# Placing the rows and the shared expert: two blocks made one, with the block words computed among the tiles

## The chip, the cores and the metric

The kernel runs on one core of one Trainium2 chip. The metric is the time of one execution on the device in microseconds (us). Five engines matter, and each works through its own queue in order: TensorE (PE, with PEld for its weight loads), VectorE (DVE), ScalarE (ACT), GpSimd (POOL) and SyncE (SP), which here only issues DMAs. They wait for each other on semaphores. A DMA issued by SP or ACT is cut into packets and spread over 16 DMA engines.

## What is computed

One decoder layer over 2048 tokens of width 1024: a mixer (sliding-window attention beside a gated recurrence), LayerNorm, then a mixture of experts with a shared expert, LayerNorm again. The change lies in the mixture, between the routing and the routed experts:

```python
    counts = jnp.bincount(flat_e, length=N_EXPERTS)
    padded = (counts + MOE_BLOCK - 1) // MOE_BLOCK * MOE_BLOCK
    pad_end = jnp.cumsum(padded)
    pad_start = pad_end - padded
    ...
    dest = pad_start[sorted_e] + (jnp.arange(n_pairs, dtype=jnp.int32) - sort_start[sorted_e])
    row_token = jnp.full((n_rows,), n_tok, jnp.int32).at[dest].set(flat_tok[order])
    block_expert = jnp.minimum(
        jnp.searchsorted(pad_end, jnp.arange(n_blocks) * MOE_BLOCK, side='right'), N_EXPERTS - 1)
    ...
    shared = (jax.nn.silu(hf @ ws_gate) * (hf @ ws_up)) @ ws_down
    return (acc[:n_tok] + shared.astype(f32)).astype(h.dtype).reshape(bsz, seq, dm)
```

Each token goes to 8 of 64 experts. The (token, expert) pairs are sorted by expert into blocks of 128 rows, each expert padded to whole blocks, at most 192 blocks.

## The kernel before

The program is a row of blocks; at the end of one all engines meet before the next begins. `mixer` takes the first 638 us, `output_and_route` the next 283 us. It leaves, per token, `mask` (the experts chosen) and `cum` (running counts), and writes the normalised rows to HBM twice: `htab` by rows (with the routing weights) and `hT_d` transposed. Behind the change stand `experts` (the routed experts, 164 blocks here) and `final_norm`.

Between them stand the two blocks that the change touches.

`place_rows` (L1202) computes positions. DVE casts `mask` and the triangle `tri` to bf16 (L1302, L1304), PE multiplies them into counts (`psCnt`) and ranks (`psRank`, L1276 to L1281), and DVE then goes through one chain of small linked operations, each waiting for the one before: block counts and ends per expert (L1308 to L1315), the block words, that is which expert each of the 192 blocks belongs to (L1317 to L1342), the position of each pair (`dm`, `d8`, `dpf`, `dbf`, `tv`, L1348 to L1359) and the table (L1365 on). Meanwhile ACT copies the shared expert's weights to rounded values `s_gu` and `s_d` in six pieces (L1291), and POOL subtracts to get the low parts, one operation for each piece (L1257). SP loads the first routed expert's weights (`prefetch_first`, 3 MB).

`shared_and_dispatch` (L1372) goes over the 16 tiles of 128 tokens with a two-deep loop (`two_deep`, L804): in the turn of tile n the engines do the head of tile n+1 and the tail of tile n. On PE a tile is 24 gate/up matmuls (L1556, high by high, high by low, low by high), the transposes of H (L1570), eight dispatch matmuls that add the token numbers into `psD` by one-hot matrices (L1574), and 12 down matmuls (L1584). On ACT: `hT_hi` (L1481), `sg` (L1491), `HT_hi` (L1496). On DVE: `hT_lo` (L1504), H (L1517), `HT_lo` (L1521), 16 one-hot operations (L1528, L1529), `out` (L1537). SP issues, in this order, the loads of `hT` for tiles 0 and 1, of `h`, the zeroing of the pad rows of `htab` and `acc` (L1442, L1443), the second routed expert's weights (`prefetch_second`, 3 MB, L1595), and only then the load of `hT` for tile 2. When the last dispatch is in, DVE writes `idx` (L1544), on which the routed experts' gathers wait.

## Time and profile before

| | |
|---|---|
| median of 3 runs | 2778.65 us (2766.59 to 2778.68) |
| profiled execution | 2779.59 us, its span 2777.4 us |
| `place_rows` in it | 921.4 to 953.3 us of the span |
| `shared_and_dispatch`, to `idx` | 953.3 to 1123.6 us |
| first matmul of the routed experts | 1132.6 us |
| TensorE busy | 2573.1 us (93%) |

Times in rows are microseconds from the start of the span unless marked ns. In a timeline row the first number is the start, the second how long the (merged) group took, then engine, line, operation, out<-in, how many, and in brackets how long the engine had been idle and who ended that. `SPq` rows are issues of DMAs. The granted clock of TensorE stands in the windows view as a share of full speed: 0.50 is 1.2 GHz, 1.00 is 2.4 GHz.

### The profile page before, as it was taken

To read this page: it belongs to the slowest core of one execution; us is meant where nothing else is said; L and a number is where in the kernel's file an instruction comes from. 1 tells how busy PE (TensorE), PEld (TensorE's weight loads), DVE (VectorE), ACT (ScalarE), POOL (GpSimd) and SP (SyncE) were. 2 spreads that over 40 slices of the span, in tenths; PEclk is the share of its full clock that TensorE was granted. 3 is DMA by queue.
4 is the path that set the end of the run, shared out by engine and by line. 5 is a ranking of instruction groups with operands and counts; after the bars stand their busy time and mean duration, and the time that the engine had idled before them with its cause. 6 is when DMAs were issued, how large, how long until landed. Compare 5 with 4: busy or idle time off the path is not lost. (4 is left out here: it accounts for less than half of the span.)

```text
span 2777.4 us, 50926 instructions
## 1 busy us (share of the span) xinstructions
PE 2573.1 (93%) x11862; PEld 1981.7 (71%) x11863; DVE 1547.3 (56%) x2691; ACT 1184.0 (43%) x1791; POOL 737.6 (27%) x825
## 2 busy tenths in 40 slices
PE   8999999997988399799999999999999999999990
PEld 4555656465777278688888888888888888888880
DVE  2544434354888667565556555565566555655535
ACT  2424343343343111454455544455555444554425
POOL 0000000001121200234344433344334333543335
PEclk9999998998999599999999999999999999999995
DMA  5010101005333444687888888789888877988656
GB/s 182 4 57 0 60 0 56 4 11 206 146 131 124 167 157 153 201 263 231 240 230 273 260 240 230 224 266 276 245 253 253 239 221 220 280 255 240 162 117 265
DMA packets 253806, 495.95 MB, mean 179 GB/s; under 512 B 24272, under 2 KB 166736, under 8 KB 253776
## 3 DMA queue, kind: packets, MB, share of 16 engines
q1 hardware_dynamic: 202816, 313.29, 32.8%
q0 software_dynamic: 47808, 179.59, 25.7%
q10 hardware_dynamic: 3152, 2.72, 0.3%
q8 instruction: 12, 0.20, 0.0%
q14 instruction: 18, 0.15, 0.0%
HBM read 366.02 MB, written 129.53 MB: 178 GB/s over the span
## 5 line engine op out<-in xcount | busy, mean ns | idle before, releaser
L1784 POOL DMA_INDIRECT acc<-y,si x164 | 293.2, 1788 | 759.5 <-DMA acc<-y,si 333.0
L1873 DVE TENSOR_TENSOR gu_lo<-raw_gu,gu_hi (+1 forms) x128 | 292.9, 2289 | 175.3 <-ACT gu_hi L1804 156.1
L1981 PE MATMUL psG<-gu_hi,xT_lo 128*128 x1320 | 348.5, 406 | 0.4 <-issue 0.3
L1970 PE MATMUL psG<-gu_hi,xT_hi 128*128 x1328 | 338.6, 397 | 3.1 <-ACT xT_hi L1800 3.1
L1970 PE MATMUL psG<-gu_lo,xT_hi 128*128 x1328 | 336.1, 395 | 0.0
L1970 PEld LDWEIGHTS psG<-gu_hi,xT_hi 128*128 128x128 f32 x1328 | 250.6, 189 | 64.1 <-issue 3.8
L1970 PEld LDWEIGHTS psG<-gu_lo,xT_hi 128*128 128x128 f32 x1328 | 250.0, 188 | 60.4
L1981 PEld LDWEIGHTS psG<-gu_hi,xT_lo 128*128 128x128 f32 x1320 | 236.7, 189 | 45.4 <-issue 1.4
L1804 ACT ACTIVATE gu_hi<-raw_gu (+1 forms) x128 | 238.3, 1910 | 45.6 <-issue 45.6
L623 PE MATMUL psP<-xT,win 128*128 128x512 f32 x512 | 236.0, 618 | 3.2 <-DMA win<-in_w_in_dram 3.2
L1760 POOL DMA_INDIRECT xg<-htab,gi x168 | 200.7, 1195 | 140.9 <-POOL gi L1757 125.8
L1873 DVE TENSOR_TENSOR d_lo<-raw_d,d_hi (+1 forms) x64 | 146.7, 2293 | 152.1 <-ACT d_hi L1804 149.4
L1853 ACT ACTIVATE HT_hi<-psH 128x256 fp32r<-128x256 f32 x164 | 63.1, 385 | 382.0 <-PE psH L1988 382.0
L1870 DVE TENSOR_TENSOR xT_lo<-psX,xT_hi 128x512 fp32r<-128x512 f32 x332 | 212.8, 683 | 8.8 <-ACT xT_hi L1800 8.7
L1942 DVE COPY y<-psY 128x512 f32<-128x512 f32 x164 | 112.9, 689 | 179.5 <-PE psY L2026 166.1
L2026 PE MATMUL psY<-d_hi,HT_hi 128*128 x656 | 207.0, 397 | 0.0
L2026 PE MATMUL psY<-d_lo,HT_hi 128*128 x656 | 206.3, 396 | 0.0
L2026 PE MATMUL psY<-d_hi,HT_lo 128*128 x656 | 206.3, 395 | 0.0
L623 PEld LDWEIGHTS psP<-xT,win 128*128 128x128 f32 x512 | 99.7, 199 | 122.9 <-issue 122.6
L1800 ACT ACTIVATE xT_hi<-psX 128x512 fp32r<-128x512 f32 x332 | 180.8, 597 | 10.4 <-PE psX L1954 1.9
L1954 PE MATMUL psX<-ident,xg 128*128 128x128 f32 x1336 | 174.1, 273 | 10.1 <-DMA xg<-htab,gi 10.1
L634 PE MATMUL psP<-win,xT 128*128 128x256 f32 (+1 forms) x512 | 171.2, 489 | 0.0
(291 smaller groups left out, 3903.4 us busy)
## 6 DMA issues: line engine op xcount, KB each, us to landing
raw_gu<-in_w_gate_dram SPq DMA_DIRECT2D x64, 1024.0 KB, 6.0
raw_gu<-in_w_up_dram SPq DMA_DIRECT2D x64, 1024.0 KB
raw_d<-in_w_down_dram SPq DMA_DIRECT2D x64, 1024.0 KB
xs<-in_x_dram SPq DMA_DIRECT2D x20, 512.0 KB, 4.2
htab<-row SPq DMA_DIRECT2D x16, 544.0 KB, 2.7
mT<-mixed SPq DMA_DIRECT2D x16, 512.0 KB, 5.4
xt<-in_x_dram SPq DMA_DIRECT2D x16, 512.0 KB, 5.8
hT_d<-hT SPq DMA_DIRECT2D x16, 512.0 KB, 3.9
```

The lines of the kernel that those rows point to most:

```text
L623: m = nc.tensor.matmul(b.tile[:], win[:, k, col:col + P], xT[:, k, :], start=(k == 0), stop=(k == KC - 1))
L634: m = nc.tensor.matmul(b.tile[:, 0:n], xT[:, k, t * P:(t + 1) * P], win[:, k, col:col + n], start=(k == 0), stop=(k == KC - 1))
L1760: nc.gpsimd.indirect_dma_start(out=xg[slot][:], out_offset=None, in_=htab, in_offset=bass.IndirectOffsetOnAxis(ap=gi[slot][:, 0:1], axis=0 ...
L1784: nc.gpsimd.indirect_dma_start(out=acc, out_offset=bass.IndirectOffsetOnAxis(ap=si[k][:, 0:1], axis=0), in_=y[k][:], in_offset=None, compu ...
L1800: nc.scalar.activation(xT_hi[slot][:, h * HALF:(h + 1) * HALF, :], psX[h][:], ACT.Copy).then_inc(xhi_s[h], 1)
L1804: nc.scalar.activation(dst, src, ACT.Copy).then_inc(done, 1)
L1870: nc.vector.tensor_tensor(xT_lo[slot][:, at, :], psX[h][:], xT_hi[slot][:, at, :], ALU.subtract).then_inc(xlo_s[h], 1)
L1873: nc.vector.tensor_tensor(dst, src, hi, ALU.subtract).then_inc(dlo_s if n == 2 else gulo_s, 1)
L1954: m = nc.tensor.transpose(psX[half][:, c, :], xg[slot][:, (half * HALF + c) * P:(half * HALF + c + 1) * P], ident[:])
L1970: nc.tensor.matmul(psG[slot][:], xT_hi[slot][:, c, :], right[:, bass.ds(w, 1), c, :].rearrange("p a n -> p (a n)"), start=(n == 0 and c == ...
L1981: m = nc.tensor.matmul(psG[slot][:], xT_lo[slot][:, c, :], gu_hi[:, bass.ds(w, 1), c, :].rearrange("p a n -> p (a n)"), start=False, stop= ...
L2026: m = nc.tensor.matmul(psY[:, h, :], left[:, c, :], right[:, bass.ds(w, 1), c, h * 512:(h + 1) * 512].rearrange("p a n -> p (a n)"), start ...
```

## The change

Both functions become one, `place_and_share`, with one block and no meeting of the engines between. The loops over the 16 tiles are written out in Python, so that the program holds all 16 tiles one after the other. The same arithmetic is done; what differs is order and place:

- DVE: `hT_lo` of tile 0 comes ahead of the expert starts, then `tri` (half as wide: the constant ones are now set on chip), then `hT_lo` of tile 1 and the positions. The block words stand behind the tiles 4 to 7, the table behind tile 9. `dm` uses the buffer of `out[1]`.
- PE: the count and rank matmuls stand ahead of the tiles; the rank matmuls wait for `tri` (`tri_s`). The dispatch of tile n-1 stands where that of tile n stood. Gate/up takes its parts as high by high, low by high, high by low, and in tile 0 waits piece by piece for the weights.
- ACT: `hT_hi` of tile 0, then the four gate/up pieces, `hT_hi` of tile 1, the two down pieces.
- SP: `hT` of tile 0 first; the pad rows are zeroed from a 64-wide column of zeros read again and again; `hT` of tiles 2 and 3 is issued ahead of `prefetch_second`; in the loop `hT` is loaded four tiles ahead.

```diff
+            load_hT(0)
+            sp.dma_start(trif[:], tri_h[:, 0, :]).then_inc(consts_in, 16)
...
+            load_hT(1)
+            load_h(0)
+            load_h(1)
+            sp.dma_start(htab[SEQ:ROWS, :].rearrange("p (a b) -> p a b", b=EXPERTS),
+                         bcast(zeros, 1, ROW_W // EXPERTS)).then_inc(pads_out, 16)
...
+            prefetch_first(sp)
+            load_hT(2)
+            load_hT(3)
+            sp.wait_ge(shared_hi_s, PIECES)
+            sp.wait_ge(shared_lo_s, PIECES)
+            prefetch_second(sp)
...
+            low(0)
+            expert_starts()
+            dve.wait_ge(consts_in, 48)
+            nc.vector.tensor_copy(tri[:], trif[:]).then_inc(tri_s, 1)
...
+            low(1)
+            positions()
+            dve.wait_ge(late_in, 48)
+            product(0)
+            for n in range(TILES):
+                if n + 2 < TILES:
+                    low(n + 2)
+                if n + 1 < TILES:
+                    product(n + 1)
+                low_HT(n)
+                one_hot(n)
+                finish(n)
+                if n == 4:
+                    ranks_of_used()
+                elif n in (5, 6):
+                    block_words(n - 5)
+                elif n == 7:
+                    codes()
+                elif n == 9:
+                    write_table()
...
+            pe.wait_ge(tri_s, 1)
...
+            gate_up(0)
+            for n in range(TILES):
+                if n + 1 < TILES:
+                    gate_up(n + 1)
+                turn_H(n)
+                if n:
+                    dispatch(n - 1)
+                if n == 9:
+                    pe.wait_ge(be_s, 1)
...
+                down(n)
+            dispatch(TILES - 1)
```

`low`, `product`, `low_HT`, `one_hot` and `finish` are the DVE steps L1504, L1517, L1521, L1528/1529 and L1537 of before.

The order on DVE where the placing begins, before (the casts, then straight into the chain; `bend` are the block ends):

```order
L1302 CAST maskb<-mask 128x1024
L1304 CAST tri<-trif 128x256
L1305 MEMSET one 128x64
L1308 TENSOR_SCALAR nbi<-psCnt 128x64
L1309 TENSOR_SCALAR nbj<-nbi 128x64
L1310 CAST nb<-nbj 128x64
L1311 SCALAR_TENSOR_TENSOR bend<-one,nb 128x64
L1313 TENSOR_SCALAR used<-nb 128x64
```

The same place on DVE after:

```order
L1506 CAST maskb<-mask 128x1024
L1507 MEMSET ones 128x128
L1508 MEMSET one 128x64
L1405 TENSOR_TENSOR hT_lo<-hT_0,hT_hi 128x1024
L1439 TENSOR_SCALAR nbi<-psC 128x64
L1440 TENSOR_SCALAR nbj<-nbi 128x64
L1441 CAST nb<-nbj 128x64
L1442 SCALAR_TENSOR_TENSOR bend<-one,nb 128x64
L1443 TENSOR_TENSOR bs<-bend,nb 128x64
L1444 TENSOR_SCALAR bst<-bs 128x64
L1512 CAST tri<-trif 128x128
L1513 CAST zr<-cum 128x192
```

The cast of `tri` has moved from the second place to the place behind six operations of the chain and the low part of tile 0.

The order on PE from the counts to the first down matmuls, before:

```order
L1276 MATMUL psCnt<-cumb,tri 128x64
L1280 MATMUL psRank<-maskb,tri 128x512
L1281 MATMUL psRank<-cumb,tri 128x512
L1280 MATMUL psRank<-maskb,tri 128x512
L1281 MATMUL psRank<-cumb,tri 128x512
L1284 MATMUL psRow<-ident,code 1x128 x2
L1207 UNCONDITIONAL_BRANCH
L1547 UNCONDITIONAL_BRANCH
L1556 MATMUL psG<-s_gu,hT_hi 128x512 x16
L1556 MATMUL psG<-s_gu,hT_lo 128x512 x8
```

And after:

```order
L1542 MATMUL psC<-cumb,ones 128x64
L1547 MATMUL psRank<-maskb,tri 128x512
L1548 MATMUL psRank<-cumb,ones 128x512
L1547 MATMUL psRank<-maskb,tri 128x512
L1548 MATMUL psRank<-cumb,ones 128x512
L1560 MATMUL psG<-s_gu,hT_hi 128x512 x8
L1560 MATMUL psG<-s_gu,hT_lo 128x512 x8
L1560 MATMUL psG<-s_gu,hT_hi 128x512 x16
L1560 MATMUL psG<-s_gu,hT_lo 128x512 x8
L1560 MATMUL psG<-s_gu,hT_hi 128x512 x8
L1570 MATMUL psH<-ident,H_0 128x128 x2
L1596 MATMUL psY<-s_d,HT_hi 128x512 x4
```

The code matmuls (`psRow`) and the meeting of the engines between ranks and gate/up are gone; the first gate/up matmul stands right behind the four rank matmuls, which read `tri`.

The order on SP around the weights of the second expert, before:

```order
L1431 DMA hT_0<-hT_d 128x1024
L1431 DMA hT_1<-hT_d 128x1024
L1434 DMA h_0<-htab 128x1024
L1434 DMA h_1<-htab 128x1024
L1442 DMA htab<-zero 128x1088
L1443 DMA acc<-zero 128x1024
L1595 DMA raw_gu<-in_w_gate_dram 128x8x256
L1595 DMA raw_gu<-in_w_up_dram 128x8x256
L1595 DMA raw_d<-in_w_down_dram 128x2x1024
L1431 DMA hT_0<-hT_d 128x1024
```

And after (the first group of three is the first expert, the second the second):

```order
L1314 DMA h_1<-htab 128x1024
L1327 DMA htab<-cum 2176x1x64
L1329 DMA acc<-cum 2048x1x64
L1619 DMA raw_gu<-in_w_gate_dram 128x8x256
L1619 DMA raw_gu<-in_w_up_dram 128x8x256
L1619 DMA raw_d<-in_w_down_dram 128x2x1024
L1308 DMA hT_0<-hT_d 128x1024
L1308 DMA hT_1<-hT_d 128x1024
L1619 DMA raw_gu<-in_w_gate_dram 128x8x256
L1619 DMA raw_gu<-in_w_up_dram 128x8x256
L1619 DMA raw_d<-in_w_down_dram 128x2x1024
L1318 DMA acc<-out_0 128x1024
```

The loads of `hT` for tiles 2 and 3 now stand ahead of the second expert's weights, but behind the first expert's and behind two zeroing transfers of 2176 and 2048 runs of 64 elements.

## Rows read from the trace of the kernel before

**Rows 1.** The page's first section: busy time of each engine.
```profile
PE 2573.1 (93%) x11862; PEld 1981.7 (71%) x11863; DVE 1547.3 (56%) x2691; ACT 1184.0 (43%) x1791; POOL 737.6 (27%) x825
```

**Rows 2.** Windows: busy time (instructions) by engine, granted clock, DMA share, GB/s.
```profile
921.40:953.30 31.90, 2.95 (x9) 0.82 (x9) 25.37 (x69) 6.80 (x7) 13.90 (x6) 0.50 0.40 134
953.30:972.90 19.60, 14.73 (x59) 11.85 (x59) 6.94 (x20) 3.79 (x4) 1.00 (x1) 0.76 0.93 328
972.90:983.50 10.60, 4.69 (x12) 3.71 (x13) 5.35 (x18) 2.55 (x4) 0.00 (x0) 0.68 0.27 107
983.50:1113.10 129.60, 129.60 (x627) 106.60 (x625) 91.47 (x263) 21.32 (x38) 0.00 (x0) 1.00 0.47 159
```

**Rows 3.** Timeline of the placing: DVE's chain beside POOL's low parts.
```profile
923.59 9.31 POOL L1257 TENSOR_TENSOR s_gu<-raw_gu,s_gu 128x1024 fp32r<-128x1024 f32 x4 [20.35 <-ACT s_gu L1291]
...
928.81 0.23 DVE L1308 TENSOR_SCALAR nbi<-psCnt 128x64 int32<-128x64 f32 x1 [0.33 <-PE psCnt L1276]
...
929.07 1.58 DVE L1309 TENSOR_SCALAR nbj<-nbi 128x64 int32<-128x64 int32 x1
...
935.38 2.17 DVE L1313 TENSOR_SCALAR used<-nb 128x64 f32<-128x64 f32 x1
...
937.91 0.22 DVE L1315 TENSOR_TENSOR bs<-bend,nb 128x64 f32<-128x64 f32 x1
```

**Rows 4.** Timeline in the routing: a DVE operation with two SBUF inputs beside POOL.
```profile
845.26 2.54 POOL L990 TENSOR_TENSOR mT_lo<-mT,mT_hi 128x1024 fp32r<-128x1024 f32 x1 [2.78 <-ACT mT_hi L1013]
...
845.59 3.29 DVE L1089 TENSOR_TENSOR row<-row,bias 128x1024 f32<-128x1024 f32 x1
```

**Rows 5.** Windows: the rank matmuls, the block words, the positions.
```profile
928.40:930.40 2.00, 1.94 (x5) 0.49 (x5) 1.63 (x4) 0.00 (x0) 2.00 (x1) 0.50 1.07 373
938.60:944.00 5.40, 0.00 (x0) 0.00 (x0) 4.70 (x20) 0.00 (x0) 0.00 (x0) 0.50 0.00 0
945.50:951.90 6.40, 0.74 (x4) 0.15 (x2) 6.06 (x26) 0.00 (x0) 0.00 (x0) 0.50 0.00 0
```

**Rows 6.** Timeline where the shared expert begins.
```profile
953.30 0.82 SPq L1431 DMA_DIRECT2D hT<-hT_d  x2
...
957.04 1.06 ACT L1481 ACTIVATE hT_hi<-hT 128x1024 fp32r<-128x1024 f32 x1 [28.79 <-DMA hT<-hT_d]
...
958.15 6.08 PE L1556 MATMUL psG<-s_gu,hT_hi 128*128 128x512 f32 x16 [11.92 <-ACT hT_hi L1481]
```

**Rows 7.** Timeline around the stall of tile 0.
```profile
965.87 2.34 SPq L1431 DMA_DIRECT2D hT<-hT_d  x2
...
977.06 1.06 ACT L1481 ACTIVATE hT_hi<-hT 128x1024 fp32r<-128x1024 f32 x1 [10.53 <-DMA hT<-hT_d]
...
978.81 2.04 PE L1584 MATMUL psY<-s_d,HT_hi 128*128 128x512 f32 x4 [5.92 <-ACT HT_hi L1496]
```

**Rows 8.** Timeline of PE in the steady loop: one tile.
```profile
1002.72 3.90 PE L1556 MATMUL psG<-s_gu,hT_hi 128*128 128x512 f32 x16
...
1009.41 1.11 PE L1584 MATMUL psY<-s_d,HT_hi 128*128 128x512 f32 x4
...
1012.22 3.90 PE L1556 MATMUL psG<-s_gu,hT_hi 128*128 128x512 f32 x16
```

**Rows 9.** Timeline of the end: last gate/up, output of tile 14, the index.
```profile
1111.06 2.03 PE L1556 MATMUL psG<-s_gu,hT_lo 128*128 128x512 f32 x8
...
1118.08 1.23 DVE L1537 SCALAR_TENSOR_TENSOR out<-h,psY 128x1024 f32<-128x1024 f32 x1
...
1123.60 0.41 DVE L1544 TENSOR_SCALAR idx<-psD,pad 128x192 int32<-128x192 f32 x1
```

**Rows 10.** DMA queues (packets, MB, share of 16 engines): 639 to 651, then 921 to 936.
```profile
q10 hardware_dynamic: 1165, 0.32, 11.8%
...
q1 hardware_dynamic: 3216, 4.43, 88.2%
```

More of the change, by code:

```diff
@@ L1475, in _ @@
-            act.dma_start(pad[:], pad_h).then_inc(consts_in, 16)
-            def high(s):
-                s.wait_slot(act, hT_in, per=16)
-                s.wait_two_behind(act, gu_s)
-                nc.scalar.activation(hT_hi[s.slot][:], hT[s.slot][:], ACT.Copy).then_inc(hThi_s, 1)
-            high(Step(0, 0))
-            def head(s):
-                if not (isinstance(s.n, int) and s.n == TILES - 1):
-                    high(s.next())
-                s.wait(act, gu_s)
-                s.wait(act, H_s, behind=1)
-                nc.scalar.activation(sg[:], psG[s.slot][:, 0:FE], ACT.Silu).then_inc(silu_s, 1)
@@ L1519, in low_HT, with link, low, product @@
-            def low_HT(s):
-                s.wait(dve, HThi_s)
+            done = [0]
+            def link(ins):
+                done[0] += 1
+                ins.then_inc(seq, 1)
+                dve.wait_ge(seq, done[0])
+            def low(n):
+                dve.wait_ge(hThi_s, n + 1)
+                nc.vector.tensor_tensor(hT_lo[n % 2][:], hT[n % 2][:], hT_hi[n % 2][:], ALU.subtract).then_inc(hTlo_s, 1)
+            def product(n):
+                dve.wait_ge(silu_s, n + 1)
+                if n >= 2:
+                    dve.wait_ge(HTps_s, n - 1)
+                nc.vector.tensor_tensor(H[n % 2][:], sg[:], psG[n % 2][:, FE:2 * FE], ALU.mult).then_inc(H_s, 1)
@@ new lines, in ranks_of_used @@
+            def ranks_of_used():
+                link(nc.vector.tensor_scalar(used[:], nb[:], 0.0, None, ALU.is_gt))
+                link(nc.vector.tensor_tensor_scan(out=rank[:], data0=one[:], data1=used[:], initial=0.0, op0=ALU.mult, op1=ALU.add))
+                link(nc.vector.tensor_scalar(last_block[:, 0:1], bend[:, EXPERTS - 1:EXPERTS], -1.0, None, ALU.add))
+                dve.wait_ge(late_in, 48)
+                link(nc.vector.tensor_scalar(bclamp[:], blockno[:], last_block[:, 0:1], None, ALU.min))
@@ new lines, in _ @@
+            nc.tensor.matmul(psC[:, 0:EXPERTS], ones[:], cumb[:, TILES, :], start=True, stop=True).then_inc(count_s, 1)
+            pe.wait_ge(tri_s, 1)
+            for hf in range(2):
+                t8 = slice(hf * 8, hf * 8 + 8)
+                o = psRank[:, t8, :].rearrange("p t e -> p (t e)")
+                nc.tensor.matmul(o, tri[:], maskb[:, t8, :].rearrange("p t e -> p (t e)"), start=True, stop=False)
+                nc.tensor.matmul(o, ones[:], cumb[:, t8, :].rearrange("p t e -> p (t e)"), start=False, stop=True).then_inc(count_s, 1)
@@ L1575, in tail, with down @@
                                          skip_group_check=True)
                 m.then_inc(disp_s, 1)
-                s.wait(pe, out_s, behind=1)
-                s.wait(pe, HThi_s)
+            def down(n):
+                if n:
+                    pe.wait_ge(out_s, n)
+                else:
+                    pe.wait_ge(shared_hi_s, PIECES)
+                    pe.wait_ge(shared_lo_s, PIECES)
+                pe.wait_ge(HThi_s, n + 1)
                 for hf in range(2):
-                    for n, (left, part) in enumerate(((HT_hi, 0), (HT_hi, 1), (HT_lo, 0))):
-                        if n == 2 and hf == 0:
-                            s.wait(pe, HTlo_s)
+                    for part, (left, right) in enumerate(((HT_hi, 0), (HT_hi, 1), (HT_lo, 0))):
+                        if part == 2 and hf == 0:
+                            pe.wait_ge(HTlo_s, n + 1)
@@ L1583, in tail @@
                         for c in range(2):
-                            m = nc.tensor.matmul(psY[:, hf, :], left[:, c, :], s_d[:, part, c, hf * 512:(hf + 1) * 512],
-                                                 start=(n == 0 and c == 0), stop=(n == 2 and c == 1))
+                            m = nc.tensor.matmul(psY[:, hf, :], left[:, c, :], s_d[:, right, c, hf * 512:(hf + 1) * 512],
+                                                 start=(part == 0 and c == 0), stop=(part == 2 and c == 1))
```

406 lines of the change are left out of this document (195 added, 211 removed).

## The prediction, made before the changed kernel was run

> **What bounds the kernel now.** The page's busy times come first: TensorE is busy for 93% of the span [rows 1], so whatever does not keep it from working is worth nothing. The windows by stage show where it is kept from working [rows 2]. In the steady loop of the shared expert, 983.5 to 1113.1, it is busy for all of 129.60 us at the full clock (1.00, 2.4 GHz): a tile costs 9.50 us, from one gate/up start to the next [rows 8], and nothing that DVE or ACT saves there can show. In the 31.9 us of the placing it works 2.95 us [rows 2]; between 972.9 and 983.5 it does 12 matmuls in 10.6 us. So there are two holes: the placing, in which everyone waits for a chain on DVE, and a stall at tile 0. The question is how early TensorE can begin the gate/up matmuls (I call that time S; it is 958.15 before [rows 6]) and how much of the road from S to the index at 1123.60 [rows 9] is kept. The index starts the routed experts, which are bound by TensorE and unchanged, so what is won there is kept to the end.
>
> **When TensorE starts now.** The first gate/up matmul stands behind the four rank matmuls, and these wait for the cast of `tri`, which DVE does behind the low part of tile 0 and six operations of the chain. So S is DVE's time for these, plus the rank matmuls. What does DVE meet there [rows 3]? While POOL makes the low parts (four pieces in 9.31 us, 2.33 us each; six pieces busy 13.90 us [rows 2]), DVE's `nbj` takes 1.58 us and ends at 930.65, `used` takes 2.17 us and ends at 937.55, where POOL has just ended its last piece; between them stand two more of the same kind. An operation that reads PSUM (`nbi`, 0.23 us at 928.81) isn't held, and once POOL is done a 128x64 operation takes 0.22 us. So beside POOL each such operation on DVE ends with POOL's present piece: one per piece. That one with two SBUF inputs is held as well is seen in the routing [rows 4]: `row<-row,bias` takes 3.29 us beside a piece of POOL that began just ahead of it. In the new order nbj, nb, bend, bs, bst and tri are six operations of these kinds, and POOL has six pieces. I take it that `tri` ends with POOL's last piece.
>
> Step by step: the load of `hT` for tile 0 is the first issue at 921.4, and `hT_hi` followed such an issue by 3.74 us [rows 6]; the stores of the routing are still under way, so 4.1: 925.5. ACT takes 1.06 for `hT_hi`, then about 1.0 for the first weight piece (six pieces are most of its 6.80 us [rows 2]): POOL starts at 927.6. Six pieces, 13.9 us: 941.5. The cast ends some 0.2 later, 941.7. The rank matmuls take 2.0 us [rows 5]: **S = 943.8**, 14.35 us earlier than before. Bounds: with the small `bs` and `bst` not held, one or two pieces less, 941.5 at the earliest of this kind; with `hT` landing 2 us later, 945.8. The middle is taken since both kinds are seen held [rows 3, 4].
>
> The positions (6.06 us of DVE work [rows 5]) follow the rank matmuls, behind the low part of tile 1, and block H of tile 0, for which TensorE asks only after the gate/up of tiles 0 and 1. Before, 59 matmuls from 958.15 ended at 972.9, of which the last ten are dispatch and turning, 1.3 us: two gate/ups at the start took 13.4 us, slow clock of the beginning included [rows 2, 6]. 6.4 us lie within that 13.4. Cost 0; without that cover it would be 6.4.
>
> **From S to the index.** Before it is 1123.60 - 958.15 = 165.45 us [rows 6, 9]. The same TensorE work is done, so I change only what differs.
>
> Stall, -7.8. ACT waits 10.53 us for the `hT` of tile 2, which landed 11 us after its issue at 965.87, behind the second expert's 3 MB, and `HT_hi` of tile 0 stands behind it on ACT; the down matmuls start at 978.81 [rows 7]. They take 2.8 us in the steady loop (1009.41 to 1012.22 [rows 8]) and here the stretch is 10.6 us [rows 2], at clock 0.68, since TensorE fell to 1.2 GHz in the wait. 10.6 - 2.8 = 7.8.
>
> Does the new order keep `hT` of tile 2 early? It must be in ACT before the gate/up of tile 1 ends, S + 13.4 - 1.06 = 956.1. From 921 on SP's queue moved 4.43 MB in 15 us, 295 GB/s [rows 10]. Now four loads of 0.52 MB stand in it as well: 6.5 MB, 22 us, 943.1; its own 0.5 MB 1.8 us: 944.9, plus P, the price of zeroing the pads in 2176 + 2048 pieces of 256 bytes, 264 for each of 16 DMA engines. No row shows writes of that size. Nearest is the queue with the router weights, 1165 packets of 275 bytes in the mean, 11.8% of 16 engines for 12 us [rows 10]: 19 ns a packet, P = 5.1. The upper end is the mean packet of the second row there (1378 bytes): 88.2% of 240 us by 3216, 66 ns, P = 17.4. I take 5.1, since the size is the same: landing at 950.0, 6.1 us early. The spare time is used up at 42 ns a packet.
>
> The Trainium skill ("DMA: Bandwidth & Descriptors", Specifications) states that below 512 bytes a DMA engine does a read-modify-write. These zeroing writes are 256 bytes, so the rule speaks against this edit; the row of small packets is a load and can't tell. If that doubled the 19 ns, P would be 10.2 and still inside the spare time; a rival below carries the case where it isn't.
>
> New gap at tile 0, +0.6: no dispatch stands between its turning and its down matmuls, and ACT's `sg` and `HT_hi` lie bare there. In all later tiles the dispatch of the tile before fills it. Code matmuls in tile 9, +0.5: in the placing they fell in a wait, now they stand in TensorE's queue; beside the positions they show as 0.74 us at clock 0.50 [rows 5], with weight loads about 1.0, halved at the full clock.
>
> Block words on DVE: 20 operations, 4.70 us [rows 5], with ranks, codes and table about 7.6 us over tiles 4 to 9. DVE is busy 91.47 of 129.60 us in the steady loop [rows 2], free 2.8 us in 9.5, some 17 us over six tiles. Behind the two heaviest tiles (2.4 us each) it is at most level. What queues behind them is the low part of a tile two ahead and H of the next, neither of which TensorE wants at once. Cost 0, bound 1; wholly bare it would be 7.6.
>
> End, +1.4. The last gate/up ended at 1113.09 and the index came 10.5 us later [rows 9]. Now DVE has the output of tile 14 (ends 1119.3, +6.2) ahead of the whole one-hot of tile 15 (about 3.9 us with `HT_lo` 4.3), and then dispatch and closing matmul (1.3): 6.2 + 4.3 + 1.3 = 11.8 to 11.9.
>
> SP's waits: the second expert's load waits for both the first expert's landing and POOL, and the store of tile 0 and the load of tile 4 queue behind it; that store is first ready near 963, the first expert landed near 950. Cost 0. Writing the loops out: no row shows a loss at the loop's edges (129.60 of 129.60), so no gain either.
>
> **Sum.** 943.8 + 165.45 - 7.8 + 0.6 + 0.5 + 1.4 = 1103.95, against 1123.60: 19.65 us less. 2779.59 - 19.65 = 2759.9 for the profiled execution. It lies 0.9 above the median of its runs, so 2759 stands for a median. A measurement of this kernel tells some 0.5% (14 us) from no change.
>
> **Rivals.**
> 1. *DVE isn't held.* The six operations take 0.3 each, `tri` is ready near 930, S = 932.0, 11.8 earlier. Then the gate/up of tile 1 ends at 945.4 and `hT` of tile 2 (950.0, due by 944.3) is late by 5.7: 11.8 - 5.7 = 6.1 more gain, 2753. Against it: four of four were held [rows 3]. For it: POOL may start later than I think.
> 2. *Small packets at 66 ns.* P = 17.4, `hT` of tile 2 lands 6.2 late, a part of the old stall returns: 2765.
> 3. *The block words are bare.* DVE's extra 7.6 us pushes TensorE: 2766.6. Against it is the free 2.8 us a tile.
> 4. *Slower: the zeroing writes cost like full packets.* 4096 bytes at 295 GB/s over 16 engines is 222 ns; 264 of them are 58.6 us, `hT` of tile 2 lands 47 us late, with ACT, H and TensorE behind it: 2759 + 47 = 2806. It is slower than before from P = 11.2 + 19.65 = 31 us on, 117 ns a packet, six times the nearest row.
>
> **How the numbers follow.** Forecast 0.78, rival 1 0.08, rival 2 0.06, rival 3 0.05, rival 4 0.03. Of the forecast's 0.78 I give 0.04 to gains below 14 us, since S may be 2 us late and the three runs of before lie 12 us apart. Faster 0.74 + 0.08 = 0.82, same 0.04 + 0.06 + 0.05 = 0.15, slower 0.03. The range takes in rivals 1 to 3 and the terms' bounds with some scatter of runs: 2746 to 2769.
>
> **What would show it.** The first gate/up matmul at about 944, right behind the rank matmuls, with PE waiting for `tri` until 941.7; DVE's six operations of about 2.3 us each beside POOL; no wait of ACT for `hT` of tile 2; tiles of 9.50 us at clock 1.00; the index near 1104. Wrong would be a first gate/up near 932, an `hT` of tile 2 landing after 956, or tiles 5 to 7 longer than 9.5.

## The result, and the profile after

The changed kernel takes **2761.58 us** in the median of 15 runs (2753.14 to 2764.11), the kernel before 2778.36 in 15 runs on the same chip: a ratio of 0.9937, 95% interval 0.9924 to 0.9951. That is some 17 us less (14 to 21 by the interval), where the prediction said 19.65. Both profiled executions say where: the span went from 2777.4 to 2758.8 us, 18.6 less, and the index from 1123.60 [rows 9] to 1104.58, 19.0 less. What follows the index takes 1654.2 us, before 1653.8, so nothing was won or lost there.

The first section of the changed kernel's page, its busy times, for [rows 1]:

```profile
PE 2568.1 (93%) x11861; PEld 1979.8 (72%) x11863; DVE 1548.6 (56%) x2691; ACT 1181.7 (43%) x1791; POOL 725.6 (26%) x824
```

TensorE's work is the same within 5 us; the span is shorter by idle time alone. The windows by stage, for [rows 2] (span and length; busy time and instructions of PE, PEld, DVE, ACT, POOL; granted clock; DMA share; GB/s):

```profile
921.60:946.20 24.60, 1.13 (x4) 0.57 (x6) 17.08 (x13) 10.07 (x10) 14.03 (x6) 0.50 1.02 312
946.20:958.90 12.70, 12.70 (x50) 10.13 (x49) 7.68 (x27) 1.33 (x2) 0.00 (x0) 0.88 0.91 314
958.90:968.40 9.50, 8.88 (x40) 6.99 (x39) 6.90 (x20) 1.60 (x3) 0.00 (x0) 1.00 0.24 78
968.40:1092.00 123.60, 123.60 (x602) 101.91 (x601) 95.59 (x294) 21.31 (x38) 0.00 (x0) 1.00 0.48 161
```

The two holes of before (31.9 and 10.6 us) have become one of 24.6 us at the start; from 946.20 on TensorE has work. The timeline of that hole, for [rows 3] and [rows 6] (start, duration, engine, line, operation, and in brackets the idle time before it with what ended it):

```profile
921.59 0.52 SPq L1308 DMA_DIRECT2D hT<-hT_d  x1
...
928.65 1.06 ACT L1365 ACTIVATE hT_hi<-hT 128x1024 fp32r<-128x1024 f32 x1 [3.60 <-DMA hT<-hT_d]
...
930.73 9.43 POOL L1351 TENSOR_TENSOR s_gu<-raw_gu,s_gu 128x1024 fp32r<-128x1024 f32 x4 [27.31 <-ACT s_gu L1382]
...
930.96 0.22 DVE L1439 TENSOR_SCALAR nbi<-psC 128x64 int32<-128x64 f32 x1
931.21 2.09 DVE L1440 TENSOR_SCALAR nbj<-nbi 128x64 int32<-128x64 int32 x1
933.34 2.28 DVE L1441 CAST nb<-nbj 128x64 f32<-128x64 int32 x1
...
942.55 2.29 DVE L1512 CAST tri<-trif 128x128 bf16<-128x128 f32 x1
...
946.23 3.54 PE L1560 MATMUL psG<-s_gu,hT_hi 128*128 128x512 f32 x8
```

`hT` of tile 0 is there 7.0 us after its issue. POOL starts a piece later, and then six operations of DVE last 2.1 to 2.4 us each where `nbi`, which reads PSUM, takes 0.22; `tri` ends with POOL's last piece. The first gate/up follows the rank matmuls at 946.23.

Tile 0, for [rows 7], and the end, for [rows 9]:

```profile
953.81 1.05 ACT L1365 ACTIVATE hT_hi<-hT 128x1024 fp32r<-128x1024 f32 x1
...
958.90 0.38 PE L1570 MATMUL psH<-ident,H 128*128 128x128 f32 x2
...
959.90 1.16 PE L1596 MATMUL psY<-s_d,HT_hi 128*128 128x512 f32 x4 [0.62 <-ACT HT_hi L1377]
...
1090.77 2.03 PE L1560 MATMUL psG<-s_gu,hT_hi 128*128 128x512 f32 x8
...
1097.81 1.21 DVE L1432 SCALAR_TENSOR_TENSOR out<-h,psY 128x1024 f32<-128x1024 f32 x1
...
1104.58 0.42 DVE L1536 TENSOR_SCALAR idx<-psRank,pad 128x192 int32<-128x192 f32 x1 [0.22 <-PE psRank L1613]
```

ACT takes `hT` of tile 2 without a wait (no bracket on its row); the down matmuls start 0.62 us after the turning; 123.60 of 123.60 us are busy at clock 1.00; and the index comes 11.8 us behind the last gate/up.

### The profile page after: what moved, and what is told of

It reads as the page before. It is cut to its first block and busy times, and to the rows that moved or that the text cites. A ratio compares the mean times of both kernels' runs of the same rounds, so it can differ in the third digit from the quotient of the medians.

```text
span 2758.8 us, 50465 instructions
## 1 busy us (share of the span) xinstructions
PE 2568.1 (93%) x11861; PEld 1979.8 (72%) x11863; DVE 1548.6 (56%) x2691; ACT 1181.7 (43%) x1791; POOL 725.6 (26%) x824
## 5 line engine op out<-in xcount | busy, mean ns | idle before, releaser
L1897 DVE TENSOR_TENSOR gu_lo<-raw_gu,gu_hi (+1 forms) x128 | 292.7, 2287 | 175.0 <-ACT gu_hi L1828 158.4
L1784 POOL DMA_INDIRECT xg<-htab,gi x168 | 190.1, 1132 | 138.8 <-POOL gi L1781 131.4
L1978 PE MATMUL psX<-ident,xg 128*128 128x128 f32 x1336 | 174.1, 274 | 8.8 <-DMA xg<-htab,gi 8.8
```

Source lines behind the costliest of these rows:

```text
L1784: nc.gpsimd.indirect_dma_start(out=xg[slot][:], out_offset=None, in_=htab, in_offset=bass.IndirectOffsetOnAxis(ap=gi[slot][:, 0:1], axis=0 ...
L1897: nc.vector.tensor_tensor(dst, src, hi, ALU.subtract).then_inc(dlo_s if n == 2 else gulo_s, 1)
L1978: m = nc.tensor.transpose(psX[half][:, c, :], xg[slot][:, (half * HALF + c) * P:(half * HALF + c + 1) * P], ident[:])
```

## The experiments

Stages ahead of this one take a few microseconds more or less from one profiled execution to the next: the first load of the stage is issued between 916.1 and 925.1 in kernels that are alike up to there. So stretches are compared. This table has them for the changed kernel and all that are built on it, in us: from that issue (`hT` of tile 0) to the first gate/up (S), from S to the index, and both together; then the ratio of the timed runs to those of before.

| kernel | issue at | to S | S to index | sum | ratio (95%) |
|---|---|---|---|---|---|
| changed kernel | 921.59 | 24.6 | 158.4 | 183.0 | 0.9937 (0.9924, 0.9951) |
| changed kernel again | 919.13 | 24.1 | 159.0 | 183.1 | 0.9928 (0.9902, 0.9954) |
| tri first | 923.96 | 9.8 | 167.3 | 177.1 | 0.9915 (0.9884, 0.9947) |
| no low parts | 922.19 | 12.1 | 164.7 | 176.8 | 0.9915 (0.9887, 0.9942) |
| words ahead | 919.74 | 24.2 | 161.9 | 186.2 | 0.9953 (0.9929, 0.9978) |
| wide zeros | 924.25 | 24.3 | 157.9 | 182.2 | 0.9944 (0.9925, 0.9962) |
| narrow zeros | 922.51 | 24.3 | 157.9 | 182.2 | 0.9916 (0.9884, 0.9948) |
| late constants | 925.07 | 18.5 | 158.4 | 176.9 | 0.9907 (0.9875, 0.9938) |
| own tile | 923.03 | 24.2 | 157.2 | 181.4 | 0.9924 (0.9899, 0.9949) |
| parts on VectorE | 916.14 | 7.3 | 166.8 | 174.1 | 0.9895 (0.9859, 0.9930) |
| the same, own tile | 916.87 | 7.1 | 166.6 | 173.7 | 0.9915 (0.9886, 0.9943) |
| the same, late second weights | 924.73 | 7.5 | 158.3 | 165.8 | 0.9849 (0.9823, 0.9874) |

Two runs of the changed kernel agree within 0.1 us in the sum and 0.6 us in its parts: from S to the first turning it takes 12.7 us in one and 13.5 in the other, for TensorE stays at half its clock for longer in the second (0.50 over the first 4.0 us, against 0.58 over the first 3.5). Differences below 1 us in one part are therefore not told from none. Moreover, the two runs with other zeros, whose sums are equal, have medians 6.7 us apart (2762.19 and 2755.50). Verdicts of a few microseconds therefore rest on the stretches, each read from one profiled execution.

**1. Is DVE held by POOL? `tri` cast first.**

```diff
-            low(0)
-            expert_starts()
             dve.wait_ge(consts_in, 48)
             nc.vector.tensor_copy(tri[:], trif[:]).then_inc(tri_s, 1)
             nc.vector.tensor_copy(zr[:]...).then_inc(zr_s, 1)
+            low(0)
+            expert_starts()
```

> The changed kernel with one move: the casts of tri and zr stand ahead of the low part of tile 0 and of the expert starts on DVE. Theory (the start of the gate/up matmuls is set by tri, which stands behind six DVE operations that POOL holds back): the rank matmuls are done by about 931.5 instead of 946.2; the gate/up of tile 0 then runs at the pace of POOL's low parts and ends near 942 instead of 953; the low part of tile 1 and the positions now end last on DVE, H of tile 0 comes at about 953.8, five us before the 958.9 of the changed kernel; index at about 1099.5 instead of 1104.6, time about 2757 (5 less than the changed kernel). Rival (something else than tri holds TensorE, the weights' low parts): tri is early, but the gate/up of tile 0 still ends near 953 and the time stays 2761.

The timeline of this run, DVE, POOL and PE at the start of the stage:

```profile
932.17 0.23 DVE L1510 CAST tri<-trif 128x128 bf16<-128x128 f32 x1 [7.25 <-DMA ident<-in_ident_h_dram]
933.05 10.00 POOL L1351 TENSOR_TENSOR s_gu<-raw_gu,s_gu 128x1024 fp32r<-128x1024 f32 x4 [27.26 <-ACT s_gu L1382]
933.78 3.97 PE L1560 MATMUL psG<-s_gu,hT_hi 128*128 128x512 f32 x8
...
943.10 2.59 PE L1560 MATMUL psG<-s_gu,hT_hi 128*128 128x512 f32 x10 [1.58 <-POOL s_gu L1351]
...
945.48 3.29 DVE L1405 TENSOR_TENSOR hT_lo<-hT,hT_hi 128x1024 fp32r<-128x1024 f32 x1
948.82 3.52 PE L1560 MATMUL psG<-s_gu,hT_lo 128*128 128x512 f32 x8 [3.13 <-DVE hT_lo L1405]
```

Ahead of POOL's first piece the same cast takes 0.23 us in place of 2.29. TensorE's first gate/up starts 14.8 us sooner, but doesn't keep that: it waits for POOL's low pieces (1.58 us) and then for the low part of tile 1 (3.13 us), which DVE, held in the chain, made late. The index is 5.9 us earlier. TensorE waits once more at the turning of tile 0, 1.34 us for H. So the held operations are real and are what bounds S; behind them POOL's 14 us of low parts is the next bound.

**2. The same from the other side: no low parts.** POOL fills the tiles with zeros instead; the low parts of the shared weights are left out of the result.

```diff
-                pool.wait_ge(shared_hi_s, n + 1)
-                nc.gpsimd.tensor_tensor(lo, raw, hi, ALU.subtract)...
+                nc.gpsimd.memset(lo.bitcast(F), 0.0)...
```

> The changed kernel, with POOL's six low parts of the shared weights replaced by six memsets to zero that wait for nothing: the low parts of the shared expert's weights are left out of the computation. Theory (POOL's two-input operations hold DVE): DVE's nbj, nb, bend, bs, bst and tri take 0.2 to 0.4 us each instead of 2.1 to 2.4, tri is ready near 933, the first gate/up matmul starts at about 934.7 instead of 946.2; then hT of tile 2 (landed at 947.9 in the changed kernel) is the next thing to be late, down matmuls of tile 0 near 950 instead of 959.9, index near 1095, time about 2752. Rival (these operations are slow by themselves or for the DMA traffic): they stay above 2 us each and the first gate/up matmul stays at 946.

The timeline of this run, two of DVE's operations, then ACT and PE at tile 0:

```profile
931.36 0.19 DVE L1439 TENSOR_SCALAR nbj<-nbi 128x64 int32<-128x64 int32 x1
...
932.63 0.23 DVE L1511 CAST tri<-trif 128x128 bf16<-128x128 f32 x1
...
949.94 1.06 ACT L1364 ACTIVATE hT_hi<-hT 128x1024 fp32r<-128x1024 f32 x1 [7.94 <-DMA hT<-hT_d]
...
951.68 2.04 PE L1595 MATMUL psY<-s_d,HT_hi 128*128 128x512 f32 x4 [4.31 <-ACT HT_hi L1376]
```

With POOL idle `nbj` takes 0.19 us and `tri` 0.23, and S comes 12.6 us earlier. This is rival 1 of the prediction, made to happen: `hT` of tile 2 is now late (ACT waits 7.94 us), and TensorE waits 4.31 us for `HT_hi` behind it. 6.4 us of the gain go back (the sum is 6.2 us shorter; this kernel's index, expected near 1095, comes at 1099.0). That is near that rival's 5.7, but made up otherwise: the wait is only 3.7 us longer than the 0.62 of the changed kernel, and the other 2.7 us are TensorE at half its clock behind it (0.50 from 951.7 to 957.0; the first four down matmuls take 2.04 us in place of 1.16), which the rival's working left out.

**3. What was the stall of tile 0 worth? The kernel before, with `hT` of tile 2 issued ahead of the second expert's weights.**

```diff
+            load(Step(0, 0))
             prefetch(sp)
-            loads_ahead(sp, TILES, load, store_and_load, store)
+            loads_ahead(sp, TILES, load, store_and_load, store, True)
```

> The kernel before with one move: the load of hT for tile 2 is issued ahead of the second expert's weights. Theory (the stall of tile 0 is the queueing of that load behind 3 MB): the wait of ACT for it, 10.5 us, is gone, the down matmuls of tile 0 start at about 973.5 instead of 978.8 and at the full clock, the index comes 7.8 us earlier (near 1116), time 7.8 below the kernel before, ratio 0.997. Rival (the stall only moves to the next load, hT of tile 3, still behind the weights): index within 2 us of 1123.6.

The timeline of this run, ACT and PE at tile 0:

```profile
973.80 1.06 ACT L1482 ACTIVATE hT_hi<-hT 128x1024 fp32r<-128x1024 f32 x1 [2.27 <-DMA hT<-hT_d]
...
977.74 1.11 PE L1585 MATMUL psY<-s_d,HT_hi 128*128 128x512 f32 x4
```

The down matmuls follow the dispatch without a gap, where they waited 5.92 us before [rows 7]. From S to the index it is 156.9 us in place of 165.45: the stall was worth 8.5 us by that stretch, and 8.2 between the turnings of tiles 0 and 1 alone (9.52 us in place of 17.67); the forecast's term was 7.8. The rival is out: the next tile takes 9.50 us, so the stall has not moved on. Of the 19 us that the change won, this one edit of a load's place would have won 8.5; the timed runs show it weakly (0.9979, 0.9957 to 1.0001).

**4. Are the block words covered? All of them ahead of the loop.**

```diff
             positions()
             dve.wait_ge(late_in, 48)
+            ranks_of_used()
+            block_words(0)
+            block_words(1)
+            codes()
             product(0)
```

> The changed kernel with the ranks, block words and codes put back ahead of the tiles, behind the positions. Theory (among the tiles they lie in DVE's free time; ahead of them only part of their 7 us finds cover under the gate/up of tiles 0 and 1): H of tile 0 at about 960.6, TensorE 1.7 to 2.2 us late at its turning, the tiles after it as before, index about 1106.6 and time about 2763.6, 2 more than the changed kernel. Rival (moving the words was the larger part of the gain): the full 7 us come back, index near 1111.5.

The timeline of this run on PE, at the turning and the down matmuls of tile 0:

```profile
958.92 0.41 PE L1568 MATMUL psH<-ident,H 128*128 128x128 f32 x2 [2.49 <-DVE H L1411]
...
959.89 2.04 PE L1594 MATMUL psY<-s_d,HT_hi 128*128 128x512 f32 x4 [0.57 <-ACT HT_hi L1377]
```

Its window (length, PE busy with instructions, granted clock, DMA share, GB/s) over those down matmuls:

```profile
959.90:962.60 2.70, 2.70 (x7) 0.50 0.00 0
```

Ahead of `product(0)` the words are bare: TensorE waits 2.49 us for H, and the down matmuls then run at clock 0.50. S to index is 3.6 us longer, 1.6 more than expected: 2.3 us lie ahead of the turning, as expected, and 1.4 between it and the next (10.84 us in place of 9.48), where the clock is low. Among the tiles they cost nothing: with them tiles 5 and 6 of the changed kernel take 9.48 and 9.49 us, the same as those without.

**5 and 6. What does a small packet cost? The pads zeroed from a tile as wide as a row, and in pieces of 64 bytes.**

```diff
-  sp.dma_start(htab[SEQ:ROWS, :]... b=EXPERTS), bcast(zeros, 1, ...))
+  sp.dma_start(htab[SEQ:ROWS, :], zero[:])                     # wide
+  sp.dma_start(htab[SEQ:ROWS, :]... b=16), bcast(zeros[:, 0:16], 1, ...))  # narrow
```

> The pads of htab and acc are written from a zero tile that is as wide as a row, so that 64 or so elements are no longer one packet of 256 bytes: 4,224 small packets become a few hundred large ones. The tile is zeroed on POOL at the start of the stage, before its low parts. Main theory (a small packet costs about 19 ns, together some 5 us of all 16 queues' time): hT of tile 2 lands 2 to 5 us earlier than the 947.85 of the changed kernel, still ahead of its use at 958, so that the time stays at 2761.6 (within 3 us); a POOL memset ahead of the low parts may cost up to 1 us at the first gate/up. Rival (a small packet costs 66 ns or more): hT of tile 2 lands over 10 us earlier. Rival (the pads cost nothing beside the loads): it lands where it did.

> The pads of htab and acc are written in pieces of 64 bytes: 16,896 packets in place of 4,224, the bytes the same. Main theory (a packet's price hardly depends on its size when it is small, about 19 ns): four times the packets are 20 us of all 16 queues' time in place of 5, so hT of tile 2 lands some 11 to 16 us later than 947.85, near or past the 958 at which it is needed, and the time is 0 to 6 us above the changed kernel (2761.6 to 2768). Rival (zeroing writes cost like full packets, 222 ns): over 200 us of the queues' time, tens of microseconds later. Rival (the price goes by bytes): nothing changes.

Packets of all queues from 915 to 975, with wide zeros:

```profile
DMA packets 7669, 14.26 MB, mean 238 GB/s; under 512 B 816, under 2 KB 5296, under 8 KB 7666
```

The same with narrow zeros; the changed kernel has 5,008 packets under 512 bytes:

```profile
DMA packets 24126, 13.56 MB, mean 226 GB/s; under 512 B 17696, under 2 KB 22176, under 8 KB 24123
```

Its timeline on ACT, the high part of tile 2:

```profile
957.92 1.06 ACT L1365 ACTIVATE hT_hi<-hT 128x1024 fp32r<-128x1024 f32 x1 [3.81 <-DMA hT<-hT_d]
```

Measured from the first issue, `hT` of tile 2 lands at 26.3 us in the changed kernel, at 24.9 with wide zeros (1.4 us sooner, where 2 to 5 was expected) and at 35.4 with narrow ones. 12,672 more packets, 792 for each of 16 DMA engines, cost 9.1 us: **11.5 ns each** at equal bytes. 4,192 packets under 512 bytes fewer save 1.4 us, 5.3 ns each, when the bytes stay. These are prices of cutting the same bytes smaller; the 19 ns of the forecast was the whole time of a packet of 256 bytes, bytes included. That is read where hardly anything else is under way. The changed kernel from 933 to 936:

```profile
DMA packets 2713, 0.69 MB, mean 231 GB/s; under 512 B 2712, under 2 KB 2712, under 8 KB 2713
```

And the narrow zeros from 937 to 943:

```profile
DMA packets 7933, 0.51 MB, mean 84 GB/s; under 512 B 7933, under 2 KB 7933, under 8 KB 7933
```

2,713 packets in 3 us on 16 engines are 17.7 ns for each of 256 bytes, and 7,933 in 6 us 12.1 ns for each of 64. So the 19 ns, read from loads of 275 bytes, held nearly for these writes, while rival 2 (66 ns) and rival 4 (222 ns) were far off. The expectation for the narrow zeros (11 to 16 us later) was too high because it kept 19 ns for a packet a fourth as long. Neither run moves the time, since even the narrow one lands just as TensorE comes to need it: S to index is 157.9 us in both. The timed ratios, 0.9944 and 0.9916, differ by less than their intervals. On the read-modify-write below 512 bytes of the Trainium skill ("DMA: Bandwidth & Descriptors", Specifications) these runs say only that such zeroing writes stay cheap here; whether one took place they can't show.

**7. Why did `hT` of tile 0 take 7.0 us? ACT's three constants issued behind the high part of tile 0.**

```diff
-            act.dma_start(iota[:], bcast(iota_h, 0, P))...
-            act.dma_start(blockno[:], blockno_h)...
-            act.dma_start(pad[:], pad_h)...
             nc.scalar.activation(cumb[:], cum[:], ACT.Copy)...
             high(0)
+            (the same three issues)
```

> ACT issues iota, blockno and pad behind the high part of tile 0 instead of ahead of it, while SP issues its own transfers; nothing else moves. It tests why hT of tile 0 took 7.0 us from issue to landing in the changed kernel, where 4.1 had been forecast. Theory (it shares queues and issue time with the constants around it): hT of tile 0 lands 1 to 3 us sooner after its issue, and the first gate/up starts 1 to 3 us sooner; time 2759 to 2761. Rival (the landing goes by the row copies and big loads that are under way anyway): the landing stays at 7 us and the time at 2761.6.

The timeline of this run, ACT, DVE and POOL at the start:

```profile
929.99 1.06 ACT L1362 ACTIVATE hT_hi<-hT 128x1024 fp32r<-128x1024 f32 x1 [3.78 <-DMA hT<-hT_d]
...
932.54 0.19 DVE L1440 TENSOR_SCALAR nbj<-nbi 128x64 int32<-128x64 int32 x1
932.82 9.28 POOL L1351 TENSOR_TENSOR s_gu<-raw_gu,s_gu 128x1024 fp32r<-128x1024 f32 x4 [25.92 <-ACT s_gu L1382]
933.00 2.34 DVE L1442 TENSOR_TENSOR_SCAN bend<-one,nb 128x64 f32<-128x64 f32 x1
...
939.89 2.29 DVE L1512 CAST tri<-trif 128x128 bf16<-128x128 f32 x1
```

The load now lands 4.9 us after its issue, 2.1 sooner. That three issues of ACT stand beside it can't be the whole cause, for in the kernel before they stood there too, and `hT` landed after 3.74 us [rows 6]. The timeline of before, ACT's issues:

```profile
953.31 0.36 ACTq L1473 DMA_DIRECT2D ident<-in_ident_h_dram  x1
953.70 0.46 ACTq L1474 DMA_DIRECT2D iota<-in_iota_h_dram  x1
```

A third, `pad`, follows at 954.18. What differs is that there the stores of the routing had long landed, and here they are under way (403 GB/s from 921.6 to 923.0, against 77 from 953.3 to 955.0). So with the stores the load takes some 1.2 us longer (4.9 against 3.74), and with stores and constants 3.3. Why the two together cost so much isn't shown.

S gains 6.1 us, three times as much, which neither theory had said. The rows show why. ACT's three issues now stand between `hT_hi` and its first weight piece, so POOL begins 2.83 us after `hT_hi` began, in the changed kernel 2.08. DVE's `nbj` begins 2.55 us after `hT_hi` in both. So here it is ahead of POOL's first piece and takes 0.19 us, `nb` too (0.20); only four operations are held, not six, and `tri` ends with POOL's fourth piece. A shift of 0.75 us between POOL's start and DVE's chain was worth two pieces of POOL. This wasn't tried by itself; the reading rests on these rows and on runs 1 and 2.

**8. Dispatch in its own tile again.**

```diff
+            one_hot(0)
             product(0)
...
                 low_HT(n)
-                one_hot(n)
+                if n + 1 < TILES:
+                    one_hot(n + 1)
...
-                if n:
-                    dispatch(n - 1)
+                dispatch(n)
```

> The dispatch of a tile stands in its own tile again, between hidden and the turn of H, with one_hot made a tile ahead; all else of the changed kernel stays. Theory (the gap of 0.6 us between the end of turn_H(0) and down(0) is there since dispatch(0) no longer fills it, and the last dispatch hangs behind the last tile): no gap at tile 0, and from the end of the last gate/up to idx 10.4 us in place of 11.8; together 2 us less, about 2759.6. Rival (a dispatch between hidden and the turn of H waits for one_hot or for the code): tiles get longer than 9.49 us, by 0.1 us each already 1.6 us in all, which eats it: 2761.6 or more.

The timeline of this run on PE, dispatch and down matmuls of tile 0:

```profile
960.41 1.05 PE L1582 MATMUL psRank<-OB,OP 128*128 128x192 f32 x8
961.30 1.11 PE L1598 MATMUL psY<-s_d,HT_hi 128*128 128x512 f32 x4
```

No gap at tile 0, tiles of 9.48 us, and the last turning is followed by the index after 6.8 us in place of 8.0. From the first turning to the index it is 144.3 us in place of 145.7 and 145.5 in the two runs of the changed kernel: 1.2 to 1.4 us gained, not 2. From the first turning to the last nothing is: 137.5 us, and 137.6 in the changed kernel. The gap that is filled takes in the work of one more dispatch within the tiles, and only the tail is won. The expectation counted both.

**9 to 11. Put together.** The first eight runs say that S is bounded by `hT` of tile 0, then by POOL; so POOL gets no work and VectorE makes the low parts, ACT the high parts ahead of `hT`.

```
 ACT  cumb, then the four gate/up high parts, high(0), high(1), two down high parts, constants
 DVE  expert_starts(), tri, zr, low_piece(0..2), low(0), low_piece(3), low(1), low_piece(4..5),
      positions() up to MAX8, product(0), rest of positions
 SP   load_hT(2), load_hT(3), pads, prefetch_first   (was pads, prefetch_first, load_hT(2), (3))
 POOL nothing
```
```diff
+            def low_piece(n):
+                dve.wait_ge(shared_hi_s, n + 1)
+                raw, hi, lo = (gu_pieces + d_pieces)[n]
+                nc.vector.tensor_tensor(lo, raw, hi, ALU.subtract).then_inc(shared_lo_s, 1)
```

> What the first eight runs point to, put together. ACT makes the high parts of the shared weights before it waits for hT of tile 0, and issues its three constants behind all of them; VectorE makes the low parts of the shared weights itself (six times 1.2 us), so that POOL has no work here and holds nobody; tri is cast and the ranks are multiplied ahead of the low parts; hT of tiles 2 and 3 is issued ahead of the pads and of the first prefetch; product(0) stands between the MAX8s and the rest of positions. Theory (the start of this stage was bounded by hT of tile 0, then by six VectorE operations held by POOL): with sc of the last routing tile at 0, hT_hi of tile 0 starts at 12.1 as in the run with late constants, or 1 to 2 us earlier, the first gate/up follows 1 us later, at 12 to 14 in place of 31.8 (25.7 with late constants), no VectorE operation takes over 1.3 us but the MAX8s, hT of tile 2 is there before gate/up(1) ends, and idx comes 15 to 18 us earlier: 2744 to 2748, ratio 0.988. What can eat it: low parts that come too late for gate/up(0) or down(0) (2 to 4 us), the slow clock after a wait (2 to 4 us). Rival (the experts' stage starts when its weights are there, not when idx is): the gain stays below 8 us, 2754 or more.

> The same, and the dispatch catches up: at tile 2 TensorE does dispatch(1) and dispatch(2), from then on each tile dispatches itself, with one_hot a tile ahead on VectorE. Theory: as above, and the tail from the last gate/up to idx is 10.4 us in place of 11.8, so 1.4 us less than the run without it, about 2743 to 2747. Rival: the second one_hot at tile 1 delays low_HT or finish there by up to 3 us, and the two come out alike.

> The changed kernel once more, on the same chip and in the same rounds as the two above, so that they can be held against it: 2761.6 us within 3, with the first gate/up 31 to 32 us behind sc of the last routing tile and idx 158 us behind the first gate/up.

The timeline of the first of these versions, ACT, DVE and PE at the start, then PE at tile 2:

```profile
921.07 1.06 ACT L1359 ACTIVATE hT_hi<-hT 128x1024 fp32r<-128x1024 f32 x1
...
921.83 0.23 DVE L1515 CAST tri<-trif 128x128 bf16<-128x128 f32 x1 [2.65 <-DMA ident<-in_ident_h_dram]
...
923.44 3.18 PE L1571 MATMUL psG<-s_gu,hT_hi 128*128 128x512 f32 x8
...
963.08 2.01 PE L1607 MATMUL psY<-s_d,HT_hi 128*128 128x512 f32 x4 [4.76 <-ACT HT_hi L1371]
```

And its waits from 945 to 1090 (who waited for what; us in total, times, longest):

```profile
ACT hT_hi L1359 <- DMA hT<-hT_d: 41.6, 12, 13.0
```

The start is as expected: no operation of DVE takes over 1.23 us, a low part takes 1.2 where POOL took 2.3, and S comes 7.3 us after the first issue, 17.3 sooner. But the index is only 8.9 us sooner, where 15 to 18 was expected, since 8.4 us come back between S and the index. From the turning of tile 2 to that of tile 3 it is 16.04 us in place of 9.5, from that of tile 0 to that of tile 1 10.89. In the first case ACT waited 13.0 us for `hT` of tile 4: SP's queue stood still from 938.0 until 946.46 before the second expert's weights, which wait for the first expert's to land, and the store of tile 0, the load of `h` and that of `hT` stood behind them, then shared the queues with 3 MB. It is the stall of [rows 7], two tiles on. In the second case `low_HT(0)` stood behind the rest of `positions`. The rival (the experts wait for weights) is wrong: they start 9 us behind the index as before. The second version, with dispatches that catch up at tile 2, has the same two stalls (17.26 and 10.89 us); its sum is 0.4 us shorter with the longer of them 1.2 us longer, so catching up would give some 1.6, where 1.4 was expected, near what one profiled execution can tell; its timed median (2752.69) can't tell that from the 2749.02 of the first.

**12. Those two stalls taken away.** The second expert's weights are issued behind the loads of tile 2, and the rest of `positions` stands behind `low_HT(0)`.

```diff
-            sp.wait_ge(shared_hi_s, PIECES)
-            sp.wait_ge(shared_lo_s, PIECES)
-            prefetch_second(sp)
             for n in range(TILES):
                 ...
                     load_hT(n + 4)
+                if n == 2:
+                    (the same two waits and the prefetch)
```

> The version with its own dispatches, with two stalls of its trace taken away: SP issues the second expert's weights behind the loads of tile 2 (there they held SP's queue until the first expert's had landed, 8 us, and hT of tile 4 then landed 13 us after its issue, so that tile 3 took 16 to 17 us in place of 9.5), and on VectorE the small operations of positions come behind low_HT(0), which they held up (down(0) waited 1.2 us, tile 0 took 10.9). Theory: no tile but the tenth is longer than 9.9 us; from the issue of hT of tile 0 to idx 165 to 167 us, where the changed kernel has 183 and the version before this one 174; 2743 to 2746, ratio to before 0.987. Rival (the second weights then collide with later loads, or the experts' stage waits for them): a tile of 13 us or more shows up after tile 2, or the first expert matmul comes more than 9 us behind idx, and the time stays at 2749 to 2753.

The timeline of this run: the first issue, the first gate/up, the index, the first matmul of the experts:

```profile
924.73 0.52 SPq L1309 DMA_DIRECT2D hT<-hT_d  x1
...
932.26 3.68 PE L1577 MATMUL psG<-s_gu,hT_hi 128*128 128x512 f32 x8
...
1090.55 0.41 DVE L1553 TENSOR_SCALAR idx<-psRank,pad 128x192 int32<-128x192 f32 x1
...
1099.57 1.97 PE L1996 MATMUL psX<-ident,xg 128*128 128x128 f32 x8 [10.11 <-DMA xg<-htab,gi]
```

165.8 us from the first issue to the index, where 165 to 167 was expected; no tile is longer than 9.6 us but the one with two dispatches (10.38) and that with the code matmuls (10.21). The median is **2737.74 us** (6 runs), the ratio to before 0.9849 (0.9823 to 0.9874): 1.5% faster than the kernel before and 0.8 to 0.9% faster than the changed kernel by medians (2761.58 and 2759.85). The stretch accounts for 17.2 us of the 22 to 24; the rest is of the size of the intervals. The two edits of this run weren't tried apart; the turnings tell them apart: that of tile 2 to that of tile 3 takes 10.38 us in place of 17.26, that of tile 0 to that of tile 1 9.42 in place of 10.89.

## Why the prediction was right

It said 2759, within 2746 to 2769; measured were 2761.58. The index was forecast at 1103.95 and came at 1104.58. Step by step:

- **S, 943.8 forecast, 946.2 found.** The mechanism held in each part: six DVE operations end with POOL's six pieces (2.1 to 2.4 us each), `tri` last; run 1 and run 2 take them away, and S comes 14.8 and 12.6 us sooner. Mis-sized is the landing of `hT` of tile 0: 4.1 us forecast, 7.0 found. The forecast had read 3.74 from [rows 6] and added 0.4 for the stores under way. Run 7 shows 4.9 without ACT's three constants and so 2.1 for them; in [rows 6] such issues stood beside the load without that price, and why they have it here is open. The forecast called 2 us more its bound; it was 2.9, and S lies outside that bound (945.8). The rank matmuls took 1.4 and not 2.0 us, which gave back a part.
- **Positions, 0.** Right: H of tile 0 is ready at 954.5, and the turning begins at 958.90, straight behind the gate/up of tile 1. Two gate/ups took 12.7 us, not 13.4 (clock 0.88 there); in the second run of the changed kernel it was 13.5.
- **Stall, -7.8.** The stall is gone, and it was worth 8.2 to 8.5 (run 3).
- **`hT` of tile 2, 950.0 forecast, 947.85 found,** due at 957.8. The price of the pads held: 17.7 ns a packet where 19 was taken, 4.7 us for P in place of 5.1. The rest is mostly the rate: from the first issue to this landing the queues moved 8.14 MB at 310 GB/s, and 295 had been taken.
- **Gap at tile 0, +0.6.** The wait is there, 0.62 us, but this term was wrong: tile 0 has also lost its own dispatch, which the sum still counts there and charges again at the end. From turning to turning tile 0 takes 9.48 us with the gap and 9.52 in run 3 without it, so the gap costs nothing. **Code matmuls, +0.5:** tile 9 takes 10.19 to 10.21 us in place of 9.49, +0.7. **Block words, 0:** right, and 3.6 us where they are bare (run 4). **End, +1.4:** 11.8 us from the last gate/up, +1.3. **SP's waits, 0:** right; the store of tile 0 is issued at 965.31, after a free queue. Run 9 shows how near that was: with S 17 us earlier the same queue costs 6.5.
- **Rival 1** is what run 2 shows, and its working (11.8 earlier, 5.7 given back) came out as 12.6 earlier and 6.4 given back. The second number is near by luck: it is 3.7 of wait and 2.7 of low clock.

The errors, +2.4 at S and -1.8 behind it (two gate/ups -0.7, gap -0.6, stall -0.4 at least, the rest small), nearly cancel: that the sum was nearer than its terms is luck, while the cause of the gain, the operations that bound S and the end of the stall, is what was forecast.

## What to carry to other kernels

Where a chain of small operations runs on VectorE beside two-input work on GpSimd, count pieces, not durations: each held operation ended with GpSimd's present piece here (those that read PSUM were not held), so put what another engine waits for ahead of the first piece, or let VectorE do the large work itself, which here took 1.2 us a piece against 2.3 on GpSimd. And where the same matmuls are only moved from one tile to another, look whether a wait takes their place before charging both. Each wait in a DMA-issuing queue holds everything behind it; a load of weights that waits belongs behind the loads of the next tiles, and each microsecond won at the start moves the next such load onto the path. Judge changes of a few microseconds by stretches of the trace that begin and end with the change, since the stages ahead of it move by more.

## What the runs showed of the hardware that was not expected

- **A load that follows stores is dear, and small loads beside it make it dearer.** A 512 KB load on quiet queues landed after 3.74 us with three small issues of ACT beside it [rows 6]; behind the stores of the routing after 4.9 without such issues (run 7) and after 7.0 with them. SP's own issues show little of it: that of `token` takes 1.23 us beside ACT's and 0.48 without, but that of `trif` 1.16 and 1.20. The mechanism is open.
- **A small write is cheap.** 17.7 ns for a packet of 256 bytes and 12.1 for one of 64, on all 16 engines at once (runs 5 and 6).
- **A long issue on SP need not be the fault of the transfer that is issued.** The timeline of SP in the changed kernel, the pads of `htab` in 2176 packets:

```profile
926.58 0.63 SPq L1327 DMA_DIRECT2D htab<-cum  x1
```

With wide zeros, the last part of the first expert's weights:

```profile
932.14 7.47 SPq L1624 DMA_DIRECT2D raw_d<-in_w_down_dram  x1
```

  The pads of `acc`, issued next in the changed kernel, take 6.27 us to issue; with wide zeros they take 0.59, but the hold has only moved to the weights. With 64-byte pieces the pads of `acc` take 10.17 us and the next issue 5.96. In that time the queue's next loads are not issued. That the hold goes by what is already queued is our reading of these rows.
- **A wait of TensorE costs more than itself.** After waits of 2.49 us (run 4) and 4.31 us (run 2) the next four down matmuls take 2.04 us in place of 1.16; the granted clock there is 0.50, 1.2 GHz, where the gate/ups before ran at 2.4 GHz. In run 2 it stays there until 957.0, and that costs 2.7 us more. A wait of 0.62 us (tile 0 of the changed kernel) left it at full speed.
